# Reordering the fill and the windows of a fused decoder step: norm applied after the projection, output stage first, sample front over two tiles, slots handled singly

## The reference, cut to what matters

```python
xn = rms_norm(x, attn_norm); proj = xn @ w_in            # (rows, 3328): q, k, v, p_rw
q, k = rope(proj[q part]), rope(proj[k part])
o_da = attend(q, k, v, lam)        # 4 heads, two softmax maps each; sample rows: 512 cached keys by page table
o_rw, wkv, shift = rwkv_time_mix(p_rw, ...)              # 8 heads of 64, a state from row to row
h = x + concat(rms_norm(o_da), o_rw) @ w_out
# peer_ffn on hn = rms_norm(h): q = hn @ wq; scores against sub_keys (8 heads x 2 x 128);
# top 16 of each half, top 16 of their 256 sums -> 128 experts a row; softmax gates
act = gelu(einsum('thkd,td->thk', u_tab[eidx], hn)); out = einsum('thk,thkd->td', gate * act, v_tab[eidx])
y = rms_norm(h + out, final_norm)
```

## Time and profile before

| | |
|---|---|
| median of 3 runs | 4260.4 us (4252.2 to 4271.9) |
| the profiled execution | 4256.6 us, span 4254.8 us |
| busy: PE, PEld, DVE, ACT, POOL | 68%, 34%, 61%, 27%, 31% of the span |
| moved | 1445.2 MB, 340 GB/s over the span |
| first expert gather | 848.5 us |
| granted TensorE clock, mean | 0.77 |

### The profile page before, as it was taken

One profiled execution on the slowest core, in us unless ns is written; L12 is line 12 of the kernel. 1 busy time (PEld: TensorE's weight loads), 2 busy tenths in 40 slices (PEclk: granted clock), 3 DMA queues, 4 the chain that ended last, 5 costly groups with the idle time before them and its releaser, 6 DMA issues.

```text
span 4254.8 us, 53587 instructions
## 1 busy us (share of the span) xinstructions
PE 2876.2 (68%) x20366; PEld 1444.2 (34%) x20366; DVE 2600.3 (61%) x5836; ACT 1141.1 (27%) x3061; POOL 1327.4 (31%) x1163
## 2 busy tenths in 40 slices
PE   4688879966667566657767676667667466655554
PEld 2544454533224223423333242333324144211111
DVE  1332165288749866883987588578838534457754
ACT  0211121133323333242333324233422122222221
POOL 0000000044424433442443243334424343245543
PEclk9889989977778678878877787877877665776555
DMA  7355714599999999999999999999999667999998
GB/s 259 129 174 190 264 36 167 197 401 384 418 380 408 401 412 367 413 416 379 404 413 414 378 404 406 403 379 413 403 364 387 207 233 270 355 364 419 419 410 347
DMA packets 319382, 1445.20 MB, mean 340 GB/s; under 512 B 28228, under 2 KB 64196, under 8 KB 179478
## 3 DMA queue, kind: packets, MB, share of 16 engines
q0 software_dynamic: 161792, 1157.70, 67.6%
q1 hardware_dynamic: 157334, 284.08, 18.7%
HBM read 1386.83 MB, written 54.85 MB: 339 GB/s over the span
## 4 chain that ended last, share of the span: by engine, by line
DMA 34%; PE 30%; DVE 23%; issue 5%; ACT 4%; POOL 3%; SPq 0%; DVEq 0%; ACTq 0%; POOLq 0%
DMA pe_buf<-in_experts,pe_idx 20%; DMA op_wkr<-scratch_wk_rows 10%; DVE pe_buf L2187 10%; PE ip_B L961 9%; PE pe_B L1292 4%; PE pe_psO L1342 4%; PE pe_B L1275 3%; POOL pe_buf L914 2%; PE pe_psH L1324 1%; PE pe_B L1246 1%; PE pe_B L997 1%; DMA tm_ps<-in_x 1%; ACT pe_Z L1644 1%; POOL at_vp L874 1%; DMA op_w<-in_w_out 1%
## 5 line engine op out<-in xcount | busy, mean ns | idle before, releaser
L914 POOL DMA_INDIRECT pe_buf<-in_experts,pe_idx x1088 | 1260.4, 1158 | 2750.4 <-PE pe_psO L1342 1717.0
L2187 DVE CUSTOM_DVE_ANT_0 pe_buf<-pe_buf,pe_hnR 128x1024 f32<-128x1024 f32 x1088 | 1315.1, 1223 | 886.3 <-DMA pe_buf<-in_experts,pe_idx 723.0
L1342 PE MATMUL pe_psO<-pe_buf,pe_Z 128*32 128x256 f32 x8704 | 791.6, 496 | 758.3 <-ACT pe_Z L1644 738.1
L1342 PEld LDWEIGHTS pe_psO<-pe_buf,pe_Z 128*32 128x32 f32 x8704 | 270.6, 131 | 1286.2 <-ACT pe_Z L1644 1014.6
L1636 ACT ACTIVATE pe_gelu<-pe_dot 128x2 f32<-128x2 f32 x544 | 110.2, 203 | 1678.1 <-DVE pe_dot L2187 1677.7
L961 PE MATMUL ip_B<-ip_w,ip_xT 128*128 128x512 f32 (+1 forms) x1008 | 421.7, 571 | 5.8 <-DMA ip_w<-in_w_in 4.0
L1324 PE MATMUL pe_psH<-pe_hn,pe_pick 128*128 128x512 f32 x544 | 404.0, 834 | 12.5 <-ACT pe_hnR L1606 11.0
L1292 PE MATMUL pe_B<-op_wkr,pe_mix 128*128 128x512 f32 (+1 forms) x576 | 294.9, 663 | 152.6 <-DMA op_wkr<-scratch_wk_rows 152.6
L1644 ACT ACTIVATE pe_Z<-pe_gl,pe_gelu 128x8 f32<-128x8 f32 x1088 | 267.7, 293 | 26.5 <-ACT pe_gelu L1636 1.8
L961 PEld LDWEIGHTS ip_B<-ip_w,ip_xT 128*128 128x128 f32 x1008 | 190.6, 193 | 210.8 <-issue 201.1
L1292 PEld LDWEIGHTS pe_B<-op_wkr,pe_mix 128*128 128x128 f32 (+1 forms) x576 | 115.6, 208 | 318.3 <-issue 317.8
(11 more groups left out here) (314 smaller groups left out, 3668.3 us busy)
## 6 DMA issues: line engine op xcount, KB each, us to landing
op_wkr<-scratch_wk_rows SPq DMA_DIRECT2D x36, 2048.0 KB, 20.8
ip_w<-in_w_in SPq DMA_DIRECT2D x24, 2048.0 KB, 8.4
op_w<-in_w_out SPq DMA_DIRECT2D x18, 2048.0 KB, 28.2
pe_buf<-in_experts,pe_idx POOLq DMA_INDIRECT x1088, 12.7
ip_w<-in_peer_wq SPq DMA_DIRECT2D x4, 2048.0 KB, 10.4
scratch_wk_rows<-ip_wkc SPq DMA_DIRECT2D x16, 512.0 KB, 3.1
tm_p<-scratch_kept_rows SPq DMA_DIRECT2D x8, 896.0 KB
out_p_all<-ip_o SPq DMA_DIRECT2D x27, 256.0 KB, 6.0
```

Of the source, the lines that this page charges most:

```text
L914: pool.indirect_dma_start(buf[b][:], None, T["experts"], bass.IndirectOffsetOnAxis(ap=idx[:, t % 2, h * NJ + j:h * NJ + j + 1], axis=0)).t ...
L1342: last = nc.tensor.matmul(psO[32 * x:32 * x + 32, j // 4, :], Z[:, n % NZ, 24 - 8 * turn:56 - 8 * turn], buf[n % NBUF][:, D + x * QUART:D ...
L2187: nc.vector.tensor_tensor_reduce(buf[b][:, 0:D], buf[b][:, 0:D], hnR[:, n // PH % 2, :], 1.0, 0.0, ALU.mult, ALU.add, dot[:, n % (NBUF):n ...
```

## The change

- The norm's factor r goes into its own tile `ip_r`, one column for each tile of rows. x is transposed unscaled; TensorE waits only for x. VectorE, after `ip_xT`, takes the reciprocal and scales the rotation table `ip_rope` of that tile; ScalarE's copies out of PSUM take r as their scale. SyncE's next load of x waits for `summed` and `scaled` as well. A tile has 3 first steps instead of 5.
- VectorE and TensorE start behind x-independent constants of their own (`first_in`: ident, attn_norm); the sums over ident and lambda are made after the first pass.
- The fill has three segments; folding comes after ip(1,2), so the first two passes load `w_in` before `peer_wq`. op(1) leaves the fill.
- A window is op(t + 1), tm(t + 2), at(t + 2); the last is op(7), tm(8), at(8), op(8) over 204 slots. New costs; the search runs over slots 42 to 122, for the sample tile over 80 to 122, and is pulled after the front steps of a slot.
- ScalarE and TensorE handle every slot by itself.

```diff
-        ((("wk", None), ("ip", (1, 2))), (("tm", 0), ("at", 0))),
-        ((("ip", (3, 4)),), (("op", 0),)),
-        ((("ip", (5, 6, 7, 8)),), (("tm", 1), ("at", 1), ("op", 1)), (("topk", 0),)))
-DURING = tuple((("tm", t), ("at", t), ("op", t)) for t in range(2, NT))
-COST = {"ip": 2.4, "wk": 1.8, "tm": 1.8, "at": 1.8, "op": 1.8, "topk": 1.8}
+        ((("ip", (1, 2)), ("wk", None), ("ip", (3, 4))), (("tm", 0), ("at", 0), ("op", 0))),
+        ((("ip", (5, 6, 7, 8)),), (("tm", 1), ("at", 1)), (("topk", 0),)))
+WK_PASS = 2
+DURING = tuple((("op", t + 1), ("tm", t + 2), ("at", t + 2)) for t in range(LAST - 2))
+DURING += ((("op", LAST - 1), ("tm", LAST), ("at", LAST), ("op", LAST)),)
+COST = {"ip": 3.3, "wk": 1.1, "tm": 1.9, "at": 1.3, "op": 2.2, "topk": 1.8}
+COST_LAST_AT = 3.3
+LAST_OP_BY = 76
-TOPK_FROM, TOPK_TO = 2, 118
+TOPK_FROM, TOPK_FROM_LAST, TOPK_TO = 42, 80, 122
...
+        length = PER if t < len(DURING) - 1 else PER + LAST_OP_BY
...
-                for _ in range(topk_pulls(k)):
-                    next(choice)
                 for _ in range(plan[n]):
                     next(front)
+                for _ in range(topk_pulls(t, k)):
+                    next(choice)
...
+                        sp.wait_ge(ip["summed"], t)
+                        sp.wait_ge(ip["scaled"], t)
...
-            pe.wait_ge(const_in, 16 * CONSTS_IN)
+            pe.wait_ge(first_in, 16 * FIRST_IN)
...
-                    pe.wait_ge(ip["scaled"], t + 1)
+                    pe.wait_ge(ip["x_in"], 16 * (t + 1))
...
-                if n >= 2 and n % 2 == 0:
-                    v_sum(n - 2)
+                if n:
                     v_sum(n - 1)
...
+                            act.wait_ge(ip["scaled"], t + 1)
+                            nc.scalar.activation(ip_o[:, g_ % 2, 0, 0:cols_of(n)], ipB[:, g_ % 3, 0:cols_of(n)], ACT.Copy,
+                                                 scale=ip_r[:, 2, t:t + 1]).then_inc(ip["copied"], 1)
...
-                if n % 2 == 1:
-                    col = (n - 1) % (NBUF)
-                    act.wait_ge(f["dotted"], n + 1)
-                    nc.scalar.activation(gelu[:, col:col + 2], dot[:, col:col + 2], ACT.Gelu_apprx_tanh).then_inc(f["gelu_done"], 1)
...
+                col = n % NBUF
+                act.wait_ge(f["dotted"], n + 1)
+                nc.scalar.activation(gelu[:, col:col + 1], dot[:, col:col + 1], ACT.Gelu_apprx_tanh).then_inc(f["gelu_done"], 1)
...
+                nc.scalar.activation(Z[:, n % NZ, 24:32], gl[:, n // PH % 2, h, :], ACT.Copy,
+                                     scale=gelu[:, col:col + 1]).then_inc(f["Z_ready"], 1)
...
-                    dve.wait_ge(ip["squared"], t + 1)
-                    chain(nc.vector.reciprocal(st[:, 2:3], st[:, 1:2]))
-                    nc.vector.tensor_scalar(ip_x[:], ip_x[:], st[:, 2:3], None, ALU.mult).then_inc(ip["scaled"], 1)
...
+                    dve.wait_ge(ip["squared"], t + 1)
+                    dve.wait_ge(ip["rope_in"], 16 * (t + 1))
+                    chain(nc.vector.reciprocal(ip_r[:, 2, t:t + 1], ip_r[:, 1, t:t + 1]))
+                    nc.vector.tensor_scalar(ip_rope[:, i].rearrange("p a d -> p (a d)"), ip_rope[:, i].rearrange("p a d -> p (a d)"),
+                                            ip_r[:, 2, t:t + 1], None, ALU.mult).then_inc(ip["scaled"], 1)
```

More of the change, by code:

```diff
@@ L175, in steps_of, with costs_of @@
     return {"wk": WK_STEPS, "tm": len(TM_LABELS), "op": OP_STEPS, "topk": TOPK_STEPS}[stage]
+def costs_of(items):
+    return [COST_LAST_AT if item == ("at", LAST) else COST[item[0]] for item in items for _ in range(steps_of(item))]
 def merged(streams):
-    left = [sum(COST[i[0]] * steps_of(i) for i in items) for items in streams]
-    costs = [[COST[i[0]] for i in items for _ in range(steps_of(i))] for items in streams]
+    costs = [costs_of(items) for items in streams]
+    left = [sum(c) for c in costs]
     spent, at = [0.0] * len(streams), [0] * len(streams)
@@ L195, in pulls @@
     plan = []
-    for t in range(LAST):
-        costs = [COST[item[0]] for item in (DURING[t] if t < len(DURING) else ()) for _ in range(steps_of(item))]
+    for t, items in enumerate(DURING):
+        costs = costs_of(items)
         total, spent, i = sum(costs), 0.0, 0
-        for k in range(PER):
+        length = PER if t < len(DURING) - 1 else PER + LAST_OP_BY
+        for k in range(length):
             n = 0
-            while i < len(costs) and spent + costs[i] <= total * min(1.0, (k + 1) / (PER - 2)) + 1e-6:
+            while i < len(costs) and spent + costs[i] <= total * min(1.0, (k + 1) / (length - 2)) + 1e-6:
                 spent, i, n = spent + costs[i], i + 1, n + 1
@@ L233, in peer @@
     ip_units = [(t, n) for tiles in passes for n in range(NG) for t in tiles]
-    loads = [("w_in", n) for n in range(NG)] + [("peer_wq", n) for n in range(NC)]
-    loads += [("w_in", n) for _ in passes[1:] for n in range(NG)]
+    loads = [("w_in", n) for _ in passes[:WK_PASS] for n in range(NG)] + [("peer_wq", n) for n in range(NC)]
+    loads += [("w_in", n) for _ in passes[WK_PASS:] for n in range(NG)]
+    wk_first, wk_base = NG * WK_PASS, NG * sum(len(tiles) for tiles in passes[:WK_PASS])
     wk_units = wk_order()
     plan = pulls()
-    CONSTS_IN, TM_CONSTS_IN = 9, 15
+    FIRST_IN, CONSTS_IN, TM_CONSTS_IN = 2, 7, 15
     NA, ND = 9, 4
@@ L593, in project @@
                         constants()
-                    for _ in range(5):
+                    for _ in range(3):
                         yield
@@ L624, in project @@
                     sp.dma_start(moved_shift, p[0:SB, :]).then_inc(ip["shift_stored"], 16)
+                if tiles == passes[WK_PASS - 1]:
                     project_stored(tiles)
@@ L936, in project @@
                         pe.wait_ge(ip["split"], split_of(base))
-                    if base and tiles == passes[1]:
+                    if tiles == passes[WK_PASS]:
                         for half in range(2):
@@ L1378, in project @@
                         act.wait_ge(ip["rotated"], rotated_of(base))
-                    nc.scalar.activation(ip_turn[:].rearrange("p a b -> p (a b)"), ip_x[:], ACT.Square, accum_out=st[:, 0:1]).then_inc(ip["summed"], 1)
+                    nc.scalar.activation(ip_turn[:].rearrange("p a b -> p (a b)"), ip_x[:], ACT.Square, accum_out=ip_r[:, 0, t:t + 1]
+                                         ).then_inc(ip["summed"], 1)
                     act.wait_ge(ip["summed"], t + 1)
-                    nc.scalar.activation(st[:, 1:2], st[:, 0:1], ACT.Sqrt, bias=eps[:, 0:1],
+                    nc.scalar.activation(ip_r[:, 1, t:t + 1], ip_r[:, 0, t:t + 1], ACT.Sqrt, bias=eps[:, 0:1],
                                          scale=1.0 / D).then_inc(ip["squared"], 1)
-                    yield
-                    yield
                     yield
@@ L1632, in slot @@
                         repeat_hn(n // PH + 1, (h - 4) // 2)
[L1633 to L1645 removed]
+                col = n % NBUF
+                act.wait_ge(f["dotted"], n + 1)
+                nc.scalar.activation(gelu[:, col:col + 1], dot[:, col:col + 1], ACT.Gelu_apprx_tanh).then_inc(f["gelu_done"], 1)
+                if h == 0:
+                    act.wait_ge(f["gl_ready"], n // PH + 1)
+                act.wait_ge(f["gelu_done"], n + 1)
+                if n >= NZ:
+                    act.wait_ge(f["v_used"], n - NZ + 1)
+                nc.scalar.activation(Z[:, n % NZ, 24:32], gl[:, n // PH % 2, h, :], ACT.Copy,
+                                     scale=gelu[:, col:col + 1]).then_inc(f["Z_ready"], 1)
                 if t and n == begin(t) + 5:
@@ L1689, in project @@
                             dve.wait_ge(ip["done"], base)
+                        if i == 0 and base >= wk_base:
                             for n in range(2):
@@ L1707, in project @@
                             dve.wait_ge(ip["done"], g_ + 1)
-                            dve.wait_ge(ip["rope_in"], 16 * (tiles[-1] + 1))
+                            dve.wait_ge(ip["scaled"], tiles[-1] + 1)
                             dve.wait_ge(ip["rotated"], rotated_of(g_))
@@ L1727, in project @@
                     if base == 0 and u == NG:
+                        constants()
                         dve.wait_ge(ip["shift_in"], 16)
```

75 lines of the change are left out of this document (32 added, 43 removed).

## The result

The changed kernel takes 4452.8 us (median of 4 runs, 4433.65 to 4457.04), the kernel before 4261.1 us (4252.23 to 4271.85): ratio 1.044, 95% interval 1.0401 to 1.0479. It is 4.4% slower. The forecast was 4217 us, inside 4155 to 4312, and faster; both are wrong. The profiled execution took 4453.2 us, its span 4451.2.

A forecast was written before the change was run, and what follows sets the result against it. TensorE was taken to bound the fill and DMA the plateau, with VectorE close behind. Terms -80 + 12 + 36 - 23 + 12 + 0 = -43 us from 4256.6, plus 3.8, gave about 4217 us; range 4155 to 4312.

The forecast's parts named there:

- Norm out of the chain: Start of the fill: TensorE's first unit starts earlier without the norm and late constants; 16 us saved, bounds 13 and 20.
- Two segments for three, and the light part: Fill: one segment boundary goes, 12 us saved; the last segment's stretch with little TensorE work shrinks, 9 us saved.
- Output stage 1: Fill: its key products, w_out products and transposes leave a TensorE-bound stretch; 43 us saved.
- Windows rotated: Six tiles: VectorE just bounds slots 42 to 122 at 98% busy; +2 us per tile, +12 in all.
- my own lower case: Rotated windows: upper time bound, VectorE at only 88% busy; +22 us per tile.
- The order within a slot: Every slot: pulling the front step ahead of the search step moves work by a slot and costs nothing.
- Slots one by one: All slots: extra gelus fall on idle ScalarE, first buffer of a pair frees sooner; 0, bounds -20 and +10.
- Sample front over two tiles, search in 42 slots, stage 7: Tiles 6 and 7: page-batch stretch -23 us, squeezed sample search +12, output stage 7 in tile 6 +36.
- C: Rival: VectorE bounds slots 42 to 122, +22 us per tile instead of +2; 4337 us, chance 0.22.
- B: Rival: page waits of the sample tile are largely absorbed, -72 us instead of -23; 4168 us, chance 0.20.
- The locked port: GpSimd gather issues: VectorE's two-port mode delays descriptors; sum stays, except up to 15 us in page batches; chance 3 in 100.

The follow-up runs named there:

- group c: Runs on one chip, where the kernel before takes 4285 us and the changed kernel 4452.6 us, ratio 1.0386.
- R: Part of the change: rotated windows, output stage 1 out of the fill, sample front over two tiles; added to F, the ratio goes from 0.9957 to 1.0096.
- O: Part of the change: a slot's front steps ahead of its search step; added to fill and rotated windows, it takes the ratio from 1.0096 to 1.0222.
- S: Part of the change: slots one by one instead of in pairs; added last, it takes the ratio from 1.0222 to 1.0386.
- F: Part of the change: norm out of the chain and two fill segments; alone on the kernel before, ratio 0.9957.
- a3: Kernel before with the fill changes, old windows and pairs, but front steps still ahead of the search step: ratio 1.0055.
- c4: Changed kernel with slots in pairs and the search step first, leaving fill, rotated windows and sample front over two tiles: ratio 1.0096.
- d3: Changed kernel with every dot product over the first 512 of 1024 elements only: 4260.2 us, ratio 1.0013.
- b1: Changed kernel with even step costs in the first six windows, as before: ratio 1.0357.
- FRS: Changed kernel with the search step again ahead of the front steps in each slot: ratio 1.0259.
- e2: Fastest kernel (short fill, old windows, search step first, single slots) with value products two slots behind the dot product instead of one: ratio 0.997.
- d1: Changed kernel with value products two slots behind the dot product instead of one, still one by one: 4399.2 us, ratio 1.0332.
- FRO: Changed kernel with slots in pairs again for gelu, gate and value products: 4387.1 us, ratio 1.0222.
- FRSO: The changed kernel with all four parts, against the kernel before: ratio 1.0386 on one chip, 1.0440 on another.
- c2: Kernel before with the fill changes alone, old windows, pairs, search step first: ratio 0.9957.
- c3: Kernel before with the fill changes and slots one by one, old windows, search step first: 4230.0 us, ratio 0.9864.
- b2: Changed kernel with the search step ahead of the front steps within a slot: ratio 1.0259.

## Why the prediction was wrong, by its own steps

On the chip of group c the change cost 168 us where the sum had -43. Of these 211 us, R has 75, the two terms that I had put at nothing (O and S) have 121 together, and F has 15.

**Norm out of the chain** (16 us): right, near its lower bound of 13. The chain of a3, whose fill starts as the change's, has the one-row load from 89.13 for 39.68 us; it lands 13.8 us earlier than in the earlier trace rows. The load itself is still there, as foreseen.

**Two segments for three, and the light part** (12 + 9 us): mis-sized. F starts its gathers 16 to 18 us earlier in all, of which 13.8 are the start; some 3 are left for both. In the changed kernel TensorE was busy 231.38 us from 243 to 518, before 239.1: no idle time came back there.

**Output stage 1** (43 us): right, 42 to 44 us (832 or 834 to 790).

**Windows rotated** (+2 per tile): wrong, and this is the first step that failed. R alone costs 86 us in tiles 0 to 5, 14 each. The step was "VectorE reaches 98%, 2.75 per slot", taken from ten microseconds of one row. With R alone (c4) slots 42 to 122 run VectorE at 88%, the value of my own lower case, and take 238 us against 220 + 6 for waits. In the changed kernel time mixing runs it at 88% too, and d3 shows that it was the bound there; attention runs it at 77%, bound by the chain shown above and not by VectorE's sum. Which piece of R costs most in these tiles (the order of the stages, the squeezed search or the new step costs) was not separated, except that even costs give back 11 us in all (b1).

**The order within a slot** ("moves work by a slot and costs nothing"): wrong, +1.0% in old windows, some +1.3% in new ones, 49 to 55 us. I argued that nothing is moved far, and not what covers what. My reading is that a search step is cover: issued ahead of the front step it fills VectorE's wait for TensorE. One such wait (for the state update of time mixing, from 800 to 3200 us) grows from 52.8 to 65.8 us when O is added to F, and from 57.5 to 80.9 when it is added to FRS. Other waits go the other way (that for attention's scores falls from 53.9 to 36.4 us in the second pair). So the cost of the order is shown, its mechanism is not.

**Slots one by one** (0, bounds -20 and +10): wrong in size and in both directions. About -1.0% in the old windows, and gone when the value products come a slot later (e2). I had seen that the first buffer of a pair comes free sooner, and put it at nothing in DMA-bound slots. +1.6% in the new ones. There TensorE gets to a front step only behind the value products of the slot just before, which wait for that slot's dot product, gelu and gate. Where front steps form a chain between engines (attention, the sample tile), the two chains are tied together; d1 loosens the tie by a slot and gets 66 us back in tiles 6 and 7. No single wait carries it: from 3500 to 3900 us the value products wait for ScalarE's gates 133.5 us in the changed kernel and 69.2 in d1, but 150.1 in c4, with pairs. In tiles 0 to 5 single slots cost some 30 us (FRO 2442, FRSO 2474), and there the slot of lag gives nothing back in sum: that part is open.

**Sample front over two tiles, search in 42 slots, stage 7** (-23 + 12 + 36 = +25): +46 with pairs (c2 to c4, 908 to 954 us for tiles 6 and 7), +84 one by one (c3 to b2, 920 to 1004). The stretch of the page batches itself went nearly as worked out with pairs: forecast 301 us for 59 slots, c4 has 307 for 59, from the wait ahead of the first batch (11.0 us) to the last; with single slots, for which I had no term, 340. The comparison was mis-sized: c2 has 250 us for its 34 slots, and the 25 slots that the stretch takes from tile 7 take 2.55 us there, not 2.75, together 314 where I had 324. So the stretch gives 7 us with pairs and not 23; the other 5 of the 21 us lie in stage 7 and the search. More slots between two batches did not hide their waits: with pairs these grow from 106.2 us (c2) to 136.2 (c4).

**The rivals.** C (VectorE bounds the rotated slots, +22 per tile, 4337 us) was the right direction and the right place, at 0.22; by "tiles over 392 us" the profile after decides for it, and with R alone slots 42 to 122 show its 88%. It has 14 of its 22 us per tile from R. The other two costs stood at zero in my sum and were no rivals at all, and the range ended at 4312. B's -72 is also more than its terms give, as far as they can be redone: 62 + 2 x 32 + 5 x 10 + 4 x 21 = 260 against 324 is -64.

**The locked port.** I had weighed the Trainium skill, "SBUF — State Buffer", section "SBUF: two separate sides", and kept it out of the sum. The runs here bear on it: in d3, with dot products of 689 ns instead of 1223, the mean gather issue on GpSimd takes 1003 ns instead of 1130, while its median hardly moves (937, 941). With that rule the traces agree in direction, at 0.13 us an issue (in which port mode the dot product runs they don't tell, and no run here separates the rule from the other differences of d3). GpSimd's issues weren't what filled its time: even in d3 it stood 1977 us waiting for buffers.

## What to carry to other kernels

An engine's share at saturation is to be read over a whole stage, not from its densest ten microseconds: here VectorE gave 88% where it was the bound and other engines' answers stood between its instructions, and 77 to 83% in a chain through three engines. Where work without dependencies shares in-order queues with a chain, its place right before the chain's wait was worth a per cent here, so "only the order in a slot changes" needs a price. And handing work over at a finer grain has two sides: buffers return sooner where DMA bounds, and queues are tied closer where a chain does; try it in the windows in which it will run.

The version to keep is the short fill with single slots, old windows and the search step first: 0.9864 and 0.9894 on two chips.

## What the runs showed that I had not expected

- The same edit (slots one by one) gave 1.1% on the kernel before and cost some 1.6% in the rotated windows.
- Taking half of the value products out took nothing off TensorE's busy time either: 857.8 us for 4488 recorded products, 868.9 for 8704. What an edit takes away is to be read from the busy time of its own row, before the total says anything.
- The gather's issue on GpSimd has a mean of 1130 ns over a median of 941 and a maximum of 4563; with half-length dot products the maximum is 2672.
